# A fused two-block model on one core: the feed-forward's ReLU and square move from VectorE to ScalarE

## The reference, cut to what matters

```python
def squared_relu_mlp(h, w_up, w_down):
    return jnp.square(jax.nn.relu(h @ w_up)) @ w_down

for l in range(DEPTH):                                   # DEPTH = 2
    ...
    x = x + gate_a * rms_norm(y, g_post_mix[l])
    h = rms_norm(x, g_pre_mlp[l]) * (1.0 + scale_m) + shift_m
    y = squared_relu_mlp(h, w_up[l], w_down[l])
    x = x + gate_m * rms_norm(y, g_post_mlp[l])
```

## Time and profile before

| | |
|---|---|
| median of 3 timed runs | 3455.35 us (3453.17 to 3459.24) |
| profiled execution, its own time | 3464.32 us |
| its span, first to last instruction | 3462.5 us |
| mean granted TensorE clock | 0.958 |
| TensorE busy | 3167.7 us (91%), 20442 matmuls |
| VectorE busy | 2562.3 us (74%), 3379 instructions |
| ScalarE busy | 1555.8 us (45%), 2207 instructions |
| HBM traffic | 770.32 MB read, 17.76 MB written |

### The profile page before, as it was taken

The page is one execution under the profiler, slowest core; times in us unless marked ns, Lnnn a source line. Parts: engine busy times, 40 slices in busy tenths (PEclk is TensorE's granted clock), DMA queues, the critical chain, the costliest instruction groups (busy, mean ns, idle before and its releaser), DMA issues.

```text
span 3462.5 us, 49687 instructions
## 1 busy us (share of the span) xinstructions
PE 3167.7 (91%) x20442; PEld 2712.5 (78%) x20442; DVE 2562.3 (74%) x3379; ACT 1555.8 (45%) x2207; POOL 0.2 (0%) x4
## 2 busy tenths in 40 slices
PE   1788889999999989999889999999899798999997
PEld 0677777888878777888678888888688687888886
DVE  7998888777878877778786766687559766656665
ACT  2355454433343455664534444444434345434343
POOL 0000000000000000000000000000000000000000
PEclk7899999999999999999899999999899999999999
DMA  9876776777778764438567666777454554454353
GB/s 365 319 273 243 267 279 243 295 300 281 293 283 310 280 230 143 173 135 309 202 233 279 227 234 235 241 263 245 161 191 164 179 184 144 171 187 153 134 183 110
DMA packets 136832, 791.32 MB, mean 229 GB/s; under 512 B 20064, under 2 KB 38624, under 8 KB 45728
## 3 DMA queue, kind: packets, MB, share of 16 engines
q1 hardware_dynamic: 107856, 755.69, 59.3%
q10 hardware_dynamic: 28752, 32.45, 2.9%
HBM read 770.32 MB, written 17.76 MB: 228 GB/s over the span
## 4 chain that ended last, share of the span: by engine, by line
PE 42%; DVE 8%; ACT 2%; DMA 2%; issue 1%; ACTq 0%; DVEq 0%
PE bk L356 41%; DVE wl L1314 2%; ACT wh L751 1%; DVE sq L1322 1%; DMA btg<-in_s_bt 1%; DMA ah<-at_keep 1%; DVE X L1314 1%; DVE pr L1314 1%; DVE raw L1322 0%; DVE Hst L1314 0%; ACT L751 0%; DVE aq L1314 0%; DVE ss L1314 0%; PE bk L360 0%; DVE hb L1314 0%
## 5 line engine op out<-in xcount | busy, mean ns | idle before, releaser
L1314 DVE TENSOR_TENSOR wl<-raw,wh 128x2048 fp32r<-128x2048 f32 x507 | 1161.3, 2291 | 406.1 <-ACT wh L751 405.7
L356 PE MATMUL bk<-HX,wh 128*128 128x512 f32 x5040 | 1278.6, 403 | 119.3 <-DVE wl L1314 62.5
L356 PEld LDWEIGHTS bk<-HX,wh 128*128 128x128 f32 x5040 | 938.6, 191 | 349.1 <-issue 109.5
L751 ACT ACTIVATE wh<-raw 128x2048 fp32r<-128x2048 f32 x507 | 966.8, 1907 | 23.9 <-DMA raw<-in_w_in 23.8
L356 PEld LDWEIGHTS bk<-HX,wl 128*128 128x128 f32 x5040 | 639.4, 190 | 34.6 <-DVE wl L1314 9.7
L356 PE MATMUL bk<-HX,wl 128*128 128x256 f32 x5040 | 652.2, 280 | 5.4 <-DVE wl L1314 5.4
L356 PE MATMUL bk<-hb,wh 128*128 128x512 f32 x2048 | 497.5, 394 | 18.5 <-ACT hb L751 9.4
L356 PEld LDWEIGHTS bk<-hb,wh 128*128 128x128 f32 x2048 | 377.0, 189 | 98.2 <-ACT hb L751 11.5
L1322 DVE SCALAR_TENSOR_TENSOR raw<-raw,cb 128x2048 f32<-128x2048 f32 x192 | 436.7, 2284 | 0.0
L356 PEld LDWEIGHTS bk<-hb,wl 128*128 128x128 f32 x2048 | 261.2, 191 | 10.6
L356 PE MATMUL bk<-hb,wl 128*128 128x256 f32 x2048 | 263.1, 281 | 0.0
(11 more groups left out here) (256 smaller groups left out, 2460.9 us busy)
## 6 DMA issues: line engine op xcount, KB each, us to landing
raw<-in_w_ada SPq DMA_DIRECT2D x192, 1024.0 KB, 5.4
raw<-in_w_up SPq DMA_DIRECT2D x128, 1024.0 KB, 4.8
raw<-in_w_down SPq DMA_DIRECT2D x128, 1024.0 KB, 4.9
raw<-in_w_in SPq DMA_DIRECT2D x74, 1024.0 KB, 5.1
raw<-in_kv_w SPq DMA_DIRECT2D x33, 1024.0 KB, 4.7
raw<-in_w_out SPq DMA_DIRECT2D x32, 1024.0 KB, 5.8
raw<-in_s_w_in SPq DMA_DIRECT2D x32, 1024.0 KB, 4.8
raw<-in_fox_w_in SPq DMA_DIRECT2D x32, 1024.0 KB, 4.8
```

Source lines behind the costliest of these rows:

```text
L356: return e.matmul(o_, l_, r_, start=start, stop=stop, skip_group_check=True)
L751: return e.activation(o_, i_, f, **kw)
L1314: return e.tensor_tensor(o_, a_, b_, op)
```

## The change

ReLU and square leave VectorE. ScalarE makes them in place in `ur` as two instructions, relu and square, inside `up_high`, ahead of the rounding copy. Each of the three waits for the one before by the semaphore `s_u2`, which now counts two per tile. VectorE keeps only the join.

```diff
             def up_high(l, j, n):
-                e.wait_ge(s_u2, 64 * l + 16 * j + n + 1)
-                act(HB[:, n, 0, :], UR[n % 2][:, :], ACT.Copy).then_inc(s_uh, 1)
+                u = UR[n % 2][:, :]
+                e.wait_ge(s_ev, up_slab(l, j, n) + 1)
+                act(u, u, ACT.Relu).then_inc(s_u2, 1)
+                e.wait_ge(s_u2, 2 * (64 * l + 16 * j + n) + 1)
+                act(u, u, ACT.Square).then_inc(s_u2, 1)
+                e.wait_ge(s_u2, 2 * (64 * l + 16 * j + n) + 2)
+                act(HB[:, n, 0, :], u, ACT.Copy).then_inc(s_uh, 1)
...
-            def up_squared(l, j, n):
-                u = UR[n % 2][:, :]
-                joined(up_slab(l, j, n), u)
-                e.wait_ge(s_ev, up_slab(l, j, n) + 1)
-                stt(u, u, 0.0, u, ALU.max, ALU.mult).then_inc(s_u2, 1)
+            def up_joined(l, j, n):
+                joined(up_slab(l, j, n), UR[n % 2][:, :])
...
-                            up_squared(l, j, n - 1)
+                            up_joined(l, j, n - 1)
...
-                            up_squared(l, j, 15)
+                            up_joined(l, j, 15)
                             up_low(l, j, 14)
                             up_low(l, j, 15)
```

## The result

The changed kernel takes 3477.8 us (median of 6 runs, 3473.7 to 3481.65), the kernel before 3455.44 us in the same comparison (6 runs): a ratio of 1.0064, with a 95% interval of 1.0051 to 1.0077. It is slower. In a second comparison it took 3478.01 us against 3461.18, ratio 1.0050 [1.0037, 1.0062]. The profiled execution took 3476.98 us, its span 3475.2, 12.7 more than before.

The account below looks back on a forecast made before the run. Taken as matmul-bound, so work counts only where TensorE waits. Ends +5.0, eighth end +0.6, transfers +6.5, S5 parameters -2.3 and clock +5.7 sum to +15.5 us; on the 3455.35 us median, 3470.9, range 3456 to 3481.

Parts of the forecast that it names:

- Inside an up half nothing: Within up halves, removed VectorE work precedes idle time and ScalarE's copy still ends 1.07 us early: no change.
- The rival of a heavier chain: ScalarE's dependent passes cost 0.55 us, not 0.43, so ends lose more: about +23 us, 3478; chance 0.15.
- the rival that VectorE's relief counts: In up halves VectorE's own queue holds the low weights, so 31 waits shrink by 0.45 us: 3446.6; chance 0.05.
- +5.0 us at five ends: At five up-half ends six serial ScalarE passes delay copy 15 by 0.99 us, paid in full by TensorE.
- the two tight ends: Two layer 1 up-half ends where slice 15 is ready just in time: 0, up to 0.3 us each if slower.
- +0.6 at the eighth end: At the last up-half end, a DMA from ScalarE's queue that holds VectorE issues 0.4 to 1.0 us later.
- +6.5 us for the late transfers: At two layer 1 places, c_keep and btg issue about 2.9 us late behind the new passes; bounds 0 to 8.
- the delay falls wholly on TensorE: TensorE already waited for btg, 1.82 and 0.89 us, so each later issue lengthens its wait by the full 2.9 us.
- -2.3 us at the S5 parameters: In layer 1's first up half VectorE is the queue, so five steps each start the low weights 0.45 us earlier.
- +5.7 us of clock: Longer TensorE gaps lower its clock, 1.9 us each at both btg stalls and one up-half end; 0 to 10.
- The base: The +15.5 us, worked out on the profiled 3464.3 us, was added to the timed median of 3455.35 us.
- It isn't what it says: ReLU or square need other tables than neighbouring copies, adding table loads, 41 us at the ends alone: about 3512; chance 0.01.

Follow-up runs that it names:

- ends_back: Kernel before with ReLU and square on ScalarE for slices 0 to 13 of each up half, 14 and 15 left on VectorE: 3464.71 us, ratio 1.0009.
- both costs away: Kernel before with the move for slices 0 to 13 only, and transfers of steps 38 and 70 ahead of ScalarE's three passes: 3461.1 us, ratio 0.9994.
- layer0_only: Kernel before with ReLU and square moved to ScalarE in the first layer only: 3470.2 us, ratio 1.0030.
- ends_only: Kernel before with ReLU and square moved to ScalarE for slices 14 and 15 of each up half only: 3475.51 us, ratio 1.0035.
- dma_first: The full change with layer 1's transfers at steps 38 and 70 issued ahead of ScalarE's three passes: 3473.82 us, ratio 1.0032 against the kernel before.

## Why the prediction held, point by point

The forecast was 3470.9 us in a range of 3456 to 3481, slower, with +15.5 us against the profiled execution. The median is 3477.8. Between medians of one comparison the change cost 22.4 us at first and 16.8 in the second; between traces 12.7 (against the first trace of before) and 16.2 (against the second). The direction and the places were right; that the sum is near is in part luck, as the terms show.

- *Inside an up half nothing.* Right. The removed instruction became 0.46 us of idle time, the copy was 1.04 us early (forecast 1.07), and `ends_back` shows it on the clock: 112 heavier slices within 0.18% of no change. The rival of a heavier chain falls with it: passes lie 0.45 us apart, where it needed 0.55. So does the rival that VectorE's relief counts.
- *+5.0 us at five ends.* The mechanism and its size were right: copy 15 at half + 2.37 (forecast 2.32), lo matmuls 1.04 later at end 1, +1.0 us in the table. At the two tight ends, between slabs 280 and 286 and 314 and 320, the distance grew by 0.3 each; in the traces that leave these ends alone it grew by -0.1 to 0.3. That is near the forecast 0, and not above 0.4.
- *+0.6 at the eighth end.* Not settled. TensorE waited there 3.98, 1.28, 4.99, 3.54 and 1.81 us in the five traces in this order where the slices 14 and 15 of layer 1 are made as before (before twice, `ends_back`, both costs away, `layer0_only`), and 3.42 and 3.53 in two pieces in the two traces of the change. Its size moves by more than the change could, so the 3.3 us of the table's sum there say nothing about the 0.6.
- *+6.5 us for the late transfers.* The step that failed in size is "the delay falls wholly on TensorE". The issue was late as forecast: half + 3.12, where I had some + 3.0; the queue did not run ahead of the waiting passes. But at the first place the transfer took 2.74 us less from issue to landing, so that it landed 18.3 us behind the half in place of 18.1. The half itself slipped by 0.4 against TensorE's slab, not 0.7, a term whose working I hadn't shown. The waits were 2.51 and 1.62 us, not about 5.4 and 3.8. At the second place chance is as large as the effect: `btg`, issued early in both traces of before, took 16.05 us to land in the first and 13.9 in the second, where TensorE didn't wait at all; with the late issue it took 13.81. There was also a third wait of 1.20 us, at step 54, where both traces of before had none. The late issue isn't its cause: `ends_only`, whose transfers go out in time, waits there 0.85 us. With the clock's part in them the three places grew by 3.9 us (4.7 against the second trace), and I had 10.3 with the clock. In `dma_first` the ratio was lower by 0.0018, against another group's 1.0050, with overlapping intervals. So the cost of the late transfers is known to a few us only.
- *-2.3 us at the S5 parameters.* -1.9, in every version that has slices 0 to 13 on ScalarE, and 0 in the others.
- *+5.7 us of clock.* Right in size only against the second trace, and elsewhere: beyond 1.0 us per end and beyond the waits for `btg`, ends and transfers cost 4.8 + 0.7 us there, and 2.3 + 1.3 against the first trace. I had 1.9 at the ends and 3.8 at the transfers. At end 4 the fall came as I let one fall; end 1 kept its clock. At end 3 the first trace of before had lost it and the second had not:

The 16 lo matmuls at end 4 of the changed kernel (2.05 us before):

```profile
1199.22 0.47 PE L356 MATMUL bk<-hb,wh 128*128 128x512 f32 x1 [0.73 <-DVE hb L1319]
1199.54 3.16 PE L356 MATMUL bk<-hb,wl 128*128 128x256 f32 x16
```

At end 3, first the second trace of before, then the change:

```profile
1006.81 1.05 PE L356 MATMUL bk<-hb,wh 128*128 128x512 f32 x2 [1.20 <-ACT hb L751]
1007.70 2.05 PE L356 MATMUL bk<-hb,wl 128*128 128x256 f32 x16
```

```profile
1010.58 0.76 PE L356 MATMUL bk<-hb,wh 128*128 128x512 f32 x1 [0.43 <-DVE hb L1319]
1011.14 3.62 PE L356 MATMUL bk<-hb,wl 128*128 128x256 f32 x16
```

So ends 3 and 4 cost 2.1 to 3.6 and 2.6 us in place of 1.0, and the one `btg` stall of 2.51 us cost 1.5 more in the matmuls behind it. With their clock the five ends cost 7.3 us against the first trace and 9.8 against the second (forecast 5.0 + 1.9), the transfers 3.9 and 4.7 (forecast 6.5 + 3.8): the two errors offset each other in the sum, which is luck.

- *The base.* I moved the sum from the trace (3464.3) to the median of three runs (3455.35). The later medians of the same kernel were 3460 to 3461, nearer to the trace; 3461 + 15.5 would have given 3476.5. But in the comparison that gave 3477.8 the kernel before took 3455.44, as I had it, and there the cost was short: 22.4 against 15.5. Whether the base or the cost made up the 6.9 us by which the forecast was short isn't known, nor is the cause of the shift between groups.
- *It isn't what it says* (table loads): nothing of it; the passes stand 0.45 us apart with nothing between them.

## What to carry to other kernels

Here, moving work from a busier to an idler engine cost nothing where there was slack and paid nothing either; its price was set by the few places without slack, the handovers between stages, and by what stood behind it in the same queue, the DMA issues. Look for these two kinds of place first. Read each wait's releaser as an edge and close the ring: the half waited for the low part, which stood behind the next weights, and putting one line ahead of another on VectorE was worth 1.3%, more than twice what the change cost. Profile the unchanged kernel twice before believing a difference of a few us.

## What the runs showed of the hardware

- A DMA in ScalarE's queue is issued while earlier arithmetic is still to run if that arithmetic's semaphores are set (half + 0.12 us), and isn't while they are not (half + 3.12). Moving it ahead of the dependent passes restored it at once.
- A late issue need not be a late landing. At the first place `btg` took 16.91, 16.49, 16.60 and 16.34 us from issue to landing when issued early (before twice, `ends_only`, `layer0_only`), 14.17 and 14.05 when issued 3 us later (the change, `ends_back`), and 13.6 when issued early but ahead of the three passes (`dma_first`). So the time of the issue alone doesn't set the landing; what else does is open. The DMA engines were full in both kernels. The stretch from the issue of `btg` to its landing, in the kernel before and then in the changed one (the last two columns are the DMA engines' busy share, 1 when all 16 are, and GB/s):

```profile
1919.00:1936.00 17.00, 15.53 (x92) 13.54 (x90) 11.97 (x15) 8.12 (x10) 0.00 (x0) 1.00 1.01 352
```

```profile
1932.00:1946.00 14.00, 11.78 (x71) 10.26 (x69) 9.13 (x12) 8.78 (x13) 0.00 (x0) 1.00 1.03 356
```

- The same gaps on TensorE don't always cost the clock: 1.33 and 0.73 us left the lo matmuls (those of `wl`) at 2.04 us at end 1, but at 3.16 and 3.22 at end 4 in the two traces of the change. In the first of them the granted clock was 1.00 over these matmuls at end 1 and 0.59 at end 4, 0.50 being the lower of its two levels (1.2 GHz). What tells them apart is open.
- ScalarE's passes of 128x256 start 0.45 us apart when each waits for the one before by a semaphore, and 0.28 to 0.33 when not (half to pass, copy to next pass): relu, square and copy took 1.31 us from the first start to the last end (628.75 to 630.06).
